# The first attention layer: its output projection in four parts, and a new order of a step's work

## The reference, cut to what matters

```python
q, k, v, qi, ki, wi = jnp.split(h @ w_in, A_SPLITS, axis=-1)      # 8 heads of 128, 2 kv heads, 8 index heads of 64
s = jnp.einsum('bqhd,bsd->bqhs', qib, ki) * IDX_DIM ** -0.5
score = jnp.einsum('bqh,bqhs->bqs', wib, jax.nn.relu(s))          # the index score
_, idx = lax.top_k(score, k_top)                                  # 128 keys per query are kept
logits = jnp.einsum('bqgrd,bqkgd->bqgrk', qg, ksel) * scale + bias
p = jax.nn.softmax(logits, axis=-1)
o = jnp.einsum('bqgrk,bqkgd->bqgrd', p, vsel)
h = h + out @ w_o                                                 # "the way out"
h = h + conv_ffn(rms_norm(h, ln_ffn_g), ...)
```

## Time and profile before

| | us |
|---|---|
| median of 3 runs | 2368.59 |
| lowest, highest | 2367.21, 2374.17 |
| the profiled execution | 2370.89 |
| span of its trace | 2369.6 |
| busy: PE, DVE, ACT, POOL | 2222.9, 1458.7, 943.5, 460.2 |

### The profile page before, as it was taken

The page is one execution under the profiler, slowest core; times in us unless marked ns, Lnnn a source line. Parts: engine busy times, 40 slices in busy tenths (PEclk is TensorE's granted clock), DMA queues, the critical chain, the costliest instruction groups (busy, mean ns, idle before and its releaser), DMA issues.

```text
span 2369.6 us, 44580 instructions
## 1 busy us (share of the span) xinstructions
PE 2222.9 (94%) x19538; PEld 1949.6 (82%) x19538; DVE 1458.7 (62%) x2296; ACT 943.5 (40%) x1600; POOL 460.2 (19%) x261
## 2 busy tenths in 40 slices
PE   4898999999988999987899999999999999999999
PEld 1677777777766777877679999999988889999987
DVE  3687888888866444398336667633355556677722
ACT  1324334334332434423554444322456654444411
POOL 0444333333310344433221000000000011000000
PEclk7899999999998999988899999999999999999999
DMA  6531011111124334310013333323311013222231
GB/s 231 135 109 54 11 42 42 42 42 42 42 87 153 99 94 125 104 45 23 10 31 108 91 92 95 90 88 99 104 48 40 19 37 116 90 90 90 85 107 67
DMA packets 57986, 184.74 MB, mean 78 GB/s; under 512 B 6944, under 2 KB 6944, under 8 KB 57792
## 3 DMA queue, kind: packets, MB, share of 16 engines
q1 hardware_dynamic: 57792, 181.89, 24.6%
HBM read 174.99 MB, written 6.88 MB: 77 GB/s over the span
## 4 chain that ended last, share of the span: by engine, by line
PE 70%; DVE 20%; ACT 6%; issue 2%; DMA 1%; POOL 0%; SPq 0%; DVEq 0%; ACTq 0%
PE PS L534 55%; DVE ca L1867 5%; PE PS L664 4%; PE PS L1018 2%; PE PS L1145 1%; PE PS L1113 1%; PE PS L859 1%; DVE Swk L2266 1%; DVE mx L2262 1%; DVE kx L1935 1%; DVE Bf L1941 1%; DVE Ssc L2242 1%; ACT Lb L1193 1%; DMA xt<-in_xT 1%; ACT tB L1193 1%
## 5 line engine op out<-in xcount | busy, mean ns | idle before, releaser
L2553 POOL TENSOR_TENSOR wlo<-raw,whi 128x1024 fp32r<-128x1024 f32 (+1 forms) x138 | 306.3, 2221 | 936.7 <-ACT whi L1193 936.7
L534 PE MATMUL PS<-nhi,whi 128*128 128x264 f32 x2064 | 441.6, 295 | 9.3 <-DVE nlo L2108 8.5
L534 PE MATMUL PS<-nlo,whi 128*128 128x264 f32 x2064 | 424.1, 288 | 0.0
L534 PE MATMUL PS<-nhi,wlo 128*128 128x264 f32 x2064 | 421.5, 286 | 0.0
L1193 ACT ACTIVATE whi<-raw 128x1024 fp32r<-128x1024 f32 (+2 forms) x306 | 303.5, 993 | 229.8 <-PE PS L534 202.0
L534 PEld LDWEIGHTS PS<-nhi,whi 128*128 128x128 f32 x2064 | 325.2, 191 | 19.6 <-DVE qB L2150 5.6
L534 PEld LDWEIGHTS PS<-nlo,whi 128*128 128x128 f32 x2064 | 325.7, 191 | 0.0
L534 PEld LDWEIGHTS PS<-nhi,wlo 128*128 128x128 f32 x2064 | 324.8, 191 | 0.0
L1779 DVE TENSOR_TENSOR wlo<-raw,whi 128x1024 fp32r<-128x1024 f32 (+1 forms) x168 | 201.1, 1197 | 171.8 <-ACT whi L1193 171.6
L534 PE MATMUL PS<-hhi,whi 128*128 128x512 f32 x648 | 263.8, 407 | 6.7 <-DVE hlo L1846 6.6
L534 PE MATMUL PS<-hhi,wlo 128*128 128x512 f32 x648 | 258.1, 398 | 2.9 <-POOL wlo L2553 2.9
(11 more groups left out here) (351 smaller groups left out, 3541.0 us busy)
## 6 DMA issues: line engine op xcount, KB each, us to landing
raw<-in_wall SPq DMA_DIRECT2D x282, 512.0 KB, 3.6
raw<-in_wall SPq DMA_DIRECT2D x32, 256.0 KB, 2.7
raw<-in_wall SPq DMA_DIRECT2D x16, 384.0 KB, 3.1
TZ<-g_rows SPq DMA_DIRECT2D x2, 2112.0 KB, 8.8
g_rows<-gsb SPq DMA_DIRECT2D x8, 328.0 KB
xt<-in_xT SPq DMA_DIRECT2D x1, 2048.0 KB, 13.4
o_rows<-os SPq DMA_DIRECT2D x8, 256.0 KB, 2.2
keep<-o_rows SPq DMA_DIRECT2D x8, 256.0 KB, 4.4
```

The costliest lines, as they stand in the source:

```text
L534: q = e.matmul(out, cuts[a][:, k * P:(k + 1) * P], (hi_, lo_)[b][:, kr, lo:lo + w], start=start and k == 0 and a == b == 0, stop=stop and ...
L2553: e.tensor_tensor(wlo[slot[i]][:, w], raw[i % NRAW][:, w], whi[slot[i]][:, w].bitcast(F32), ALU.subtract).then_inc(*up("lo_pool", i))
```

## The change

- The way out is four parts of two heads, each 8 units of 2 steps. Three parts (24 units, 48 `g`) lie between the attention steps; the last (8 units, 16 steps) stays in `residual`. The adds to H are 24 and 8 instead of 8 and 8.
- In a pass TensorE transposes step n-2 first and applies step n-3 after it. ScalarE takes the exponential of step n ahead of the scaling of step n-1, both in the second token, then its copy to `PT`. VectorE takes the maximum of step n ahead of the reciprocal of step n-1.
- `FIRST` is 4, and the `PT` copies of these four steps are all ScalarE's (`by_act`).
- VectorE's part of the index score has a token of its own, `d`, apart from `s`; `rel` has four buffers.
- What was put off runs at step 5 of an `a_in` unit, step 0 of an `a_out` unit (`b_kv` and `b_out` stay at 3 and 1).
- `SELECT` is written anew, with 184 `g`.

The diff, cut:

```diff
-FIRST = 5
-SELECT = ("g" * 16 + 3 * "gggggsggg" + "ggsgggsggsg" + 2 * "gsgrgrgsgrgrgsgr" + "gsgrgsgrgsgrgsgr" + "grgrgrgrgggg"
-          + "grgrgrgrgrgrgraagr" + 4 * "grgragrgrgrgrgraagr" + "gar" + 3 * "aagag" + 9 * "aaga" + 8 * "aaa"
-          + 3 * ("aagag" "aagag" "aagag" "aaga" "aaga") + 4 * "aagga")
+FIRST = 4
+SELECT = ("g" * 16 + 3 * "gggsggdggg" + "gsggdgrgrgrgrgr" + "grgrgrsgrgrdggg" + "sgrgrdgrsgrdgggg" + "sgrgrdgrgrgggg"
+          + 2 * "sgrgrdsgrgrdsgrdgrgg" + "sgrgrdsgrgrdgrgrgraag" + "grgragrgrgrgrgraagr" + 2 * "grgragrgrgrgrgraag"
+          + "ga" + 3 * ("aaga" "aaga" "aagag") + 3 * "aaga" + 7 * "aagag" + 2 * "aaga" + 3 * ("aagag" "aaga" "aagag") + "aaga"
+          + 7 * "aagag" + 2 * "aaga")
...
-    for k0 in (0, 4):
+    for k0 in range(0, 8, 2):
         for j in range(8):
-            units.append(("a_out", j * P, k0, 4))
+            units.append(("a_out", j * P, k0, 2))
...
-        rel = grid(blockmem("rel", 2 * T), 2)
+        rel = grid(blockmem("rel", 4 * T), 4)
...
+        def by_act(name, n):
+
+            return n < FIRST if name == "a" else n % 2 == 0
...
-                    if k == (1 if what in ("a_out", "b_out") else 3):
+                    if k == {"a_in": 5, "b_kv": 3, "a_out": 0, "b_out": 1}[what]:
                         flush()
...
-                for j in range(8):
-                    b = pair_of_banks(("res_a1", j))
-                    yield from steps_of("a_out", b, ohi_a, olo_a, (lambda k: on.wait_ge(*at("oa", k))) if j == 0 else None)
-                    yield
+                for p in range(3):
+                    for j in range(8):
+                        b = pair_of_banks(("res_a1", p, j))
+                        yield from steps_of("a_out", b, ohi_a, olo_a, (lambda k: on.wait_ge(*at("oa", k))) if j == 0 else None, 2 * p)
+                        yield
...
                     if n < N:
                         scores(n)
                     yield
+                    if 2 <= n <= N + 1:
+                        turn(n - 2)
+                    yield
                     if 3 <= n <= N + 2:
                         apply(n - 3)
                     yield
-                    if 2 <= n <= N + 1:
-                        turn(n - 2)
-                    yield
...
-            residual("a_out", "res_a", ohi_a, olo_a, "oa", first=4)
+            residual("a_out", "res_a", ohi_a, olo_a, "oa", first=6)
...
-                            if h >= 2 or i < 3:
-                                on.wait_ge(*at("score", i if h >= 2 else i + 1, (h - 2) % 8))
-                            act(sv(rel[:, n, 0:w], w), psv(w, first[n]), ACT.Relu, scale=0.125).then_inc(*up("rel", i, h))
+                            if h >= 4 or i < 3:
+                                on.wait_ge(*at("score", i if h >= 4 else i + 1, (h - 4) % 8))
+                            act(sv(rel[:, h % 4, 0:w], w), psv(w, first[n]), ACT.Relu, scale=0.125).then_inc(*up("rel", i, h))
...
                 for n in range(N + 4):
+                    yield
+                    if n < N:
+                        on.wait_ge(*at("a_neg", n))
+                        act(row(n), row(n), ACT.Exp, bias=cell(n, 1), accum_out=cell(n, 2)).then_inc(*up("a_exp", n))
                     if 1 <= n <= N:
                         on.wait_ge(*at("a_inv", n - 1))
                         act(row(n - 1), row(n - 1), ACT.Copy, scale=cell(n - 1, 2)).then_inc(*up("a_weights", n - 1))
+                    if 2 <= n <= N + 1:
+                        turn(n - 2)
                     yield
...
                 for n in range(N + 4):
+                    if n < N:
+                        scores(n)
+                    yield
                     if 1 <= n <= N:
                         on.wait_ge(*at("a_exp", n - 1))
                         e.reciprocal(cell(n - 1, 2), cell(n - 1, 2)).then_inc(*up("a_inv", n - 1))
-                    if n < N:
-                        scores(n)
-                    yield
-                    yield
                     if 2 <= n <= N + 1:
                         turn(n - 2)
+                    yield
...
-            run(SELECT, a=attend_a(), s=select(), r=rounds(), g=made_a())
+            run(SELECT, a=attend_a(), s=nothing(), d=select(), r=rounds(), g=made_a())
```

More of the change, by code:

```diff
@@ L895, in tensor, with steps_of @@
             later.append(first_stats)
[L897 to L900 removed]
+            def steps_of(what, b, hi_, lo_, rhs=None, k0=0):
+                for k, _ in enumerate(product(what, hi_, lo_, halves(T, b), rhs, k0=k0)):
+                    if k == {"a_in": 5, "b_kv": 3, "a_out": 0, "b_out": 1}[what]:
                         flush()
@@ L1525, in made_a @@
                         yield
-                for j in range(8):
-                    yield from steps_of(4, 1)
+                for _ in range(24):
+                    yield from steps_of(2, 0)
                     yield
@@ L2218, in made_a @@
                         yield
-                for j in range(8):
-                    b = a_pair()
-                    yield from steps_of(4, 1)
-                    i = count.take()
-                    on.wait_ge(*at("unit", i))
-                    if j == 0:
-                        on.wait_ge(*at("H_scaled", 7))
-                    e.tensor_tensor(sv(H[:, j, :], T), psv(T, b), sv(H[:, j, :], T), ALU.add).then_inc(*up("res_a1", j))
-                    ahead(i + 3)
-                    yield
+                for p in range(3):
+                    for j in range(8):
+                        b = a_pair()
+                        yield from steps_of(2, 0)
+                        i = count.take()
+                        on.wait_ge(*at("unit", i))
+                        on.wait_ge(*(at("res_a1", p - 1, j) if p else at("H_scaled", 7)))
+                        e.tensor_tensor(sv(H[:, j, :], T), psv(T, b), sv(H[:, j, :], T), ALU.add).then_inc(*up("res_a1", p, j))
+                        ahead(i + 3)
+                        yield
             def select():
@@ L2392, in ffn @@
                 residual(f"ffn{layer}", gname, gj, 3, last=gname is None)
-            residual("res_a", "ln_ffn_g_2", 0, 1, after="res_a1")
+            residual("res_a", "ln_ffn_g_2", 0, 1, after=("res_a1", 2))
             ffn(0, "ln_attn_g_2", 8)
@@ L2535, in vector @@
             run("g" * 16 + 8 * BESIDE + AFTER, a=attend(), g=made_beside())
-            residual("res_b", "ln_ffn_g_2", 8, 1, after="res_b1")
+            residual("res_b", "ln_ffn_g_2", 8, 1, after=("res_b1",))
             ffn(1)
@@ L2656, in made_a @@
                 while units[count.next][0] in ("a_in", "a_out"):
-                    nk = units[count.next][3]
-                    if nk == 4 and units[count.next][2]:
+                    what, _, k0, nk = units[count.next]
+                    if what == "a_out" and k0 == 6:
                         return
@@ L2696, in attend_a @@
                     yield
-            run(SELECT, a=attend_a(), s=nothing(), r=rounds(), g=made_a())
+            run(SELECT, a=attend_a(), s=nothing(), d=nothing(), r=rounds(), g=made_a())
             while units[count.next][0] != "b_kv":
```

40 lines of the change are left out of this document (16 added, 24 removed).

## The result

| | before | after |
|---|---|---|
| median of five runs each, us | 2369.56 (2367.21 to 2374.17) | 2360.85 (2359.74 to 2362.81) |
| span of the profiled execution, us | 2369.6 | 2361.5 |
| ratio of the times, 95% interval | | 0.9959 [0.9944, 0.9973] |

The change makes the kernel 8.7 us faster by the medians, 8.1 by the spans, where 4.7 was forecast. That is past the bound of 0.3% (7.1 us), though the interval of the ratio reaches to both sides of it.

A forecast was written before the change was run, and what follows sets the result against it. TensorE, busy 94%, was taken as the bound, with VectorE setting the end of the selection. Net of the selection and the stretch -3.1, way out -3.1, clock +1.5: -4.7 us, 2363.9; range 2353 to 2374.

The forecast's parts named there:

- collisions: In the selection, VectorE work falling clear of GpSimd's `wlo`: gain 0 to 6 us, 2.5 taken.
- Part 1: Selection: ends near 1106.7 instead of 1118.9, 12.2 us earlier.
- Rival C: In the selection, accumulations clear GpSimd altogether: 3.5 us more, 2360.4; chance 0.10.
- Part 2: Selection's end to last apply: last apply ends at 1239.7 against 1242.8, 3.1 us won.
- Waits: TensorE's waits from selection's end to last apply, mostly for ScalarE's PT copies: 9 us, bounds 3 and 20.
- Clock: Clock loss from selection's end to last apply: 1.5 us, bounds 0 and 9.9, since every pass has fillers.
- rival B: At the selection's end TensorE is not ahead, held by later scores of wide heads: +5, 2368.9; chance 0.18.
- Part 3: Last part of the way out: last apply to first `residual` add 3.0 us instead of 6.1, 3.1 won.
- The ring: First `residual` add to last `nlo`: eight adds hang on one another, and these 27.7 us stay.
- A: Selection's end onward: waits of 3 us instead of 9, no clock lost anywhere; -13.7, 2354.9; chance 0.18.
- D: In the passes, ScalarE's copy chain runs late: waits 26 us, not 9; +17, 2380.9; chance 0.12.
- E: Way out: unsplit heads make TensorE wait at `oa`, or low clock runs into `up0`; +3, 2366.9; chance 0.06.

The follow-up runs named there:

- experiments 4: Changed kernel with ScalarE's PT copy ahead of the exponential in the first six passes only; 2356.3 us, ratio 0.9945 to the kernel before.
- 12: Changed kernel with VectorE's low parts of weights behind the add in the residual parts, and ScalarE's PT copy early in the first six passes; 2347.67 us, ratio 0.9901.
- 7: Changed kernel with reciprocal again ahead of maximum on VectorE and scaling ahead of exponential on ScalarE; 2358.03 us, ratio 0.9944.
- 11: Changed kernel with VectorE's low parts behind the add in the residual parts, and VectorE's and ScalarE's old inner orders; 2349.6 us, ratio 0.9909.
- Experiments 1: Changed kernel with the old order of a pass on TensorE, ScalarE and VectorE; 2372.2 us, ratio 1.0006 to the kernel before.
- 9: Kernel before with only the new order of a pass on all three engines; 2368.23 us, ratio 0.9992.
- experiment 2: Changed kernel with the old tokens up to the last round and FIRST = 5; 2370.35 us, ratio 1.0002 to the kernel before.
- Experiment 3: Changed kernel with only heads 0 to 3 of the way out between the steps, 16 fillers fewer there; 2364.95 us, ratio 0.998 to the kernel before.
- experiment 5: Changed kernel with VectorE's low parts of the next weights behind the add in both layers' residual parts; 2354.53 us, ratio 0.9927 to the kernel before.

## Why the prediction was right and where it was not

The direction, the range and the outline held: an earlier selection, most of it eaten by the quarter moved in, a shorter way from the last apply to the first add, and a ring that nearly stays. That the sum came so near is partly luck: collisions won 5.2 us more than forecast and the clock cost 5.2 more, and smaller errors offset each other too. The time came 3.1 us below the forecast of 2363.9 (by the gain 3.4 in the spans, and 4.0 in the medians of five, in which the kernel before is at 2369.56), past the bound at which it counts as faster, to which 0.38 was given. Step by step:

- **Part 1, the selection.** 12.2 us forecast, 15.3 measured. The mis-sized term is the collisions: 2.5 taken of "0 to 6"; the groups above show 10.2 won less 2.5 given back at the `mask`, 7.7. The argument with which I took the low end ("where VectorE stands against GpSimd isn't set by the order of tokens") is what failed. The other terms together come to 7.6 against 9.7. The size of the collision term isn't a property of the order alone: experiments 4 and 12, whose programs are the same up to the last apply, end the selection at 1102.5 and 1104.2, and 7 and 11 at 1100.6 and 1101.5. Rival C, with 0.10 and 2360.4, came nearest in time, but not in what happened: the 21 accumulations of 400, 272 and 144 columns won 3.2 us of the 10.2 (16.4 to 13.2), the rest came from other instructions, and one accumulation still takes 2.46 us in the changed kernel.
- **Part 2, the stretch.** 133.0 us forecast, 134.2 measured, but made of other parts. TensorE's own work: 122.5 forecast; busy 127.2 less half of the 13.4 busy us between 1105 and 1121 is 120.5. Waits: 9 forecast, 7.0 of holes measured (the waits listed sum to 9.6, since matmuls overlap their ends), and not spread over six wide steps at 1.3 to 1.7 each and the even steps behind them: one of 5.6, and hardly any other. Clock: 1.5 forecast "since every pass has fillers", 6.7 measured, all in one piece behind that hole. I had placed the hole rightly, at the apply behind a wide step's transposes with ScalarE's copy late, but did not follow ScalarE's queue back: its exponential waits for a maximum that stands behind the rounds. Experiment 4 takes the copy out of that queue and wins 4.6 us by the medians, 3.3 by the ratios. The errors (2.0 less work, 2.0 less of waits, 5.2 more of clock) offset each other but for 1.2.
- **The order of a pass** got no term of its own, only "the old 11.2 us should mostly go". Experiments 1, 7 and 9 give it 11.3 us, none of it by the inner orders, and only together with the rest of the change. It and the earlier selection (9.5, experiment 2) each cancel the quarter's price; without either the change would have been rival B, nothing.
- **Fillers and clock.** The prediction counted 19 more product steps at 0.74 as a cost and set the old holes and the old clock loss against them as sums of their own. Experiment 3 shows the exchange directly: even sixteen of the steps, taken from passes that had two, earn more than they cost, 17.1 us of holes and clock against 11.8 of work.
- **Part 3.** The gap: 3.0 forecast, 3.7 measured. The split is 0.98 for `olo_a` instead of the 0.7 or so that I had in 1.4 with the add (0.69 is the median of the eight; a GpSimd `wlo` started at 1239.20 beside this one), and step 7 stands 0.96 us for it. The ring: 27.7 forecast to stay, 26.9 measured, links of 2.81 instead of 2.92. With units of 4 steps there again experiment 3 has 2.92 and 27.7, so the units' length is in the ring after all, with 0.8 us. Clock in it: 1.5 forecast as a cost; it did fall, to 0.50 from 1261.8 to 1265.2 (the 0.68 above is the mean of 5 us), but TensorE waits for VectorE there anyway, and the last `nlo` was not later. This term should have been nothing; its upper bound of 3.4 isn't what two stretches like the earlier trace rows give either (half of 4.21 busy us, twice: 4.2). The holes are 8.5 us, not 12. That the ring is VectorE's was right, that it "stays" was not a law: experiment 5 takes 4.7 us out of it.
- **Rivals.** A (2354.9) had the clock wrong, D (slower, ScalarE's copy chain) had the right engine but the chain is late once, not in every pass: 6.5 us of waits against the 20.8 from which it decides. B did not happen: TensorE stood at its apply from 1101.07 on, before the selection ended. E did not happen: `oa` costs 1 us.

Sum by the marks: 1.8 more at the last apply, 0.7 less in the gap, 0.8 in the ring, 1.5 of clock not paid: 3.4 us.

## What to carry to other kernels

Where TensorE waits behind another engine's queue, look at the stretch at half clock that may follow; here it cost 6.7 us after a wait of 5.6, though its length varied between runs. And follow the queue back to the instruction that holds it, as here from the copy to an exponential to a maximum behind the rounds. A new order of dependent steps and the fillers between them are one change: here the order was worth 1.8 us without the rest and 11.3 with it, so count the two together. Where one engine's small instructions form a ring, look for long ones that stand inside it by the order of a helper and not by need.

## What was not expected of the hardware

- After one hole of 5.64 us TensorE's clock stood at 0.50 (1.2 GHz) for 17.1 us, with TensorE busy 13.4 of the 16 us from 1105 to 1121; after one of 5.2 us in experiment 7 it stood there for 6.8, after waits of 2.2, 0.7 and 0.5 in experiment 4 for 10.2. No row explains these lengths, and the program alone doesn't set them: experiments 4 and 12 are the same up to the last apply and stood low for 10.2 and 3.4 us. Nor is half of the low time always what it costs: between these two holes of 5.1 and 6.4 us took part of it back, and the stretch is 1.1 us shorter, not 3.4.
- The clock also stayed low under full work: in experiment 9 at 0.50 from 1163.6 to 1183.3, TensorE being busy 10.00 of the 10 us from 1165 to 1175.
- A VectorE TENSOR_SCALAR with one tensor input and 400 columns took 2.60 us beside a GpSimd `wlo` and 0.42 alone, and a two-input instruction of 144 columns 2.41 and 0.37: both ended about when the `wlo` did (2.36 and 2.35 us).
